# Three moves in a two-layer decoder step: an output panel's upper half between two copies, sample numerators on two column tiles, and the eighth sum of squares with its column sums later

## The chip, the cores and the metric

The kernel runs on one core of a Trainium2 chip, as one launch. The metric is the device time of that launch in microseconds (us); lower is better. One profiled execution gives the durations below; it has its own time, which is not exactly the median of the timed runs.

The engines are named as in the profile: PE (TensorE, with PEld for its weight loads), DVE (VectorE), ACT (ScalarE), POOL (GpSimd) and SP (which here issues DMAs). Each runs its own list of instructions in order and waits on semaphores for the others.

## The reference

Two layers for 512 prompt tokens and 64 sample tokens (8 sequences of 8), model width 1024, in fp32. Layer 0 mixes with multi-head latent attention, layer 1 with a chunkwise mLSTM of 4 heads. Around each mixer stand two half-step feed-forward layers (four in all, width 2816), then a gated per-layer embedding. Cut to what the change touches:

```python
for i in range(DEPTH):                       # 2 layers, both token groups
    x = x + 0.5 * swiglu(rmsnorm(x, g_ffa[i]), w_ffa_in[i], w_ffa_out[i])
    h = rmsnorm(x, g_mix[i])
    x = x + (latent_attention(h) if i == 0 else mlstm(h))
    x = x + 0.5 * swiglu(rmsnorm(x, g_ffb[i]), w_ffb_in[i], w_ffb_out[i])
    gate = sigmoid(rmsnorm(x, g_ple[i]) @ w_ple_gate[i])
    x = x + gate * (p[i] @ w_ple_proj[i])

# swiglu:  a, b = split(h @ w_in); (silu(a) * b) @ w_out
# rmsnorm: x * rsqrt(mean(x * x) + 1e-6) * g
# mlstm, per head, for the 8 sample sequences b of 8 tokens each:
#   num = (S * decay) @ [v, 1] + (q * decay_b) @ [C_b, n_b]     # 64 tokens x 257
```

The last line is what part B below is about: each sample sequence has its own state of 128 x 257, and its 8 tokens alone meet it.

## The kernel before

**Layout.** Tokens lie along the free axis (T = 576), channels on the 128 partitions in 8 chunks. Every fp32 product of weights and activations is made of three: weights and activations are split into an upper half (a rounding to fp32r, made by ACT's `Copy`) and a remainder (`raw - upper`, made by DVE or POOL), and PE multiplies upper x upper, upper x remainder and remainder x upper (lines 2461, 2463, 2466 for panels; 2523, 2524, 2525 for the blocks of the feed-forward's input product).

**Feed-forward.** `Part` cuts the 22 column chunks of the hidden width into three parts (6, 8 and 8 chunks), for each of four feed-forwards. For one chunk `pair(...)` on PE makes seven block products (`block_product`, 12 multiplications of 288 columns each) that form the gate and the value column tile by a Strassen-like scheme; `w_done` counts them. Between them ACT copies intermediate sums from one PSUM bank to another (`copied`, four for a chunk, after block products 1, 2, 3 and 5); the seventh block product waits for the fourth copy, the fifth for the third. Behind the sixth DVE adds and scales (L2181, L2184), ACT takes the silu (L1844), DVE multiplies the two halves (L2169), ACT makes the upper half of the result (L1837) and DVE the remainder (L2173).

After the last chunk of a part come the part's eight output tiles (`out_tile`): tile k needs panel `part.p + k` of `w_out` in its two halves, `whi` (ACT, L1794 through `upper`) and `wlo` (POOL for k = 0 and 1, L1739; DVE for the others). `raw` has 4 slots for panels as they come from memory, `whi` and `wlo` have 2 each. ACT's queue in the part's last chunk, before: copy 1, upper half of the chunk before, copy 2, copy 3, copy 4, then the upper half of panel 0 (it waits for its load, `raw_ready`, and for the slot), then the silu. The upper half of panel 1 stands behind the silu and the last chunk's upper half.

**Between a mixer or the embedding and the next feed-forward** (`added`, and `ple` of layer 0), DVE adds each of 8 tiles to x, prepares the blocks of x for the block products (`x_blocks`) and adds ACT's squares into `acc` (`x_sum`, L2114); four third remainders (`x_third_lower`, L2290) and the fourth weight block's (`fourth_lower`, L2161) end it. PE needs the third remainders in block product 5. `token_sums` on PE (L2474, five columns, ten passes) sums `acc` over the partitions when all eight sums are in; DVE's `means` (L2091), POOL's power (L1750) and PE's `spread` (L2482, after block product 7) make the norm of it.

**mLSTM heads.** For each of 4 heads PE runs four prompt numerators (L1563), a gate panel (24 x 2 multiplications; not in the last head), the stabilisers (L1532 to L1534), the sample numerators (L1573 and L1575), then states (L1582), the prompt state (L1589), the next head's scores (L1548) and turns. DVE copies each numerator (L1404), makes the denominators and carries the states (L1409); ACT squares the copied numerators (L1248) behind the next head's exponentials (L1229, L1231).

In `qdm` each of the 8 sequences has a block of 64 columns, in which only its own 8 tokens are not zero: sequence b has tokens 8b to 8b + 7. A multiplication of one block with state `Cb[:, b, :]` adds into all 64 partitions of the bank, 56 of them zeros.

The functions that the diff touches:

## Time and profile before

| | us |
|---|---|
| median of 3 runs | 2567.34 (2565.26 to 2567.75) |
| the profiled execution | 2565.75 |
| its span | 2563.8 |
| PE busy | 2473.5 (96%) |
| DVE busy | 1684.0 (66%) |
| ACT busy | 1073.0 (42%) |
| POOL busy | 307.7 (12%) |

The granted clock of PE was 0.989 of full speed on the mean, and DMA moved 84 GB/s. The profile's page gives shares over the whole span, the chain of waits follows the end of the program back to its start, and the timeline shows the instructions of one engine in order: start, duration, engine, line, operation, what is written and read, and in brackets how long the engine stood idle before it and what ended that. Equal instructions that follow each other are one row (x16); the duration of a multiplication's row runs to its modelled end, so the step from one row's start to the next is the time that it took.

### The profile page before, as it was taken

What the parts mean: (1) busy time and instruction counts of PE and PEld (TensorE: products, weight loads), DVE (VectorE), ACT (ScalarE), POOL (GpSimd) and SP (SyncE); (2) the same over time, 40 slices, a digit from 0 to 9 for tenths busy, and PEclk for the clock granted to TensorE, in tenths of its full rate; (3) what the DMA queues carried; (4) which work ended last, traced back from release to release, by engine and by line L of the source; (5) the groups of instructions that cost most, each with busy time, mean ns of one, the idle gap of its engine ahead of it and who ended that gap; (6) DMA issues with size and microseconds to landing.
All of it is one profiled execution on the core that took longest, in us unless ns stands there. A gap on an engine that the chain in (4) does not pass through costs nothing.

```text
span 2563.8 us, 45161 instructions
## 1 busy us (share of the span) xinstructions
PE 2473.5 (96%) x17653; PEld 2355.3 (92%) x17653; DVE 1684.0 (66%) x2398; ACT 1073.0 (42%) x1780; POOL 307.7 (12%) x247
## 2 busy tenths in 40 slices
PE   6999999999899999999998999999999999999998
PEld 5999999877688999999998999999997789999998
DVE  6676675888555586848568585765434586857666
ACT  6444353455333453525445353443133354443532
POOL 0000001202330100000030000001322200000012
PEclk9999999999899999999999999999999999999999
DMA  4233232222232222333222333332323222332322
GB/s 121 83 99 91 83 94 78 52 49 75 72 110 77 58 79 87 99 87 94 84 78 78 91 91 91 90 91 71 92 69 103 87 66 82 99 99 82 96 76 72
DMA packets 410806, 216.44 MB, mean 84 GB/s; under 512 B 40085, under 2 KB 407834, under 8 KB 410650
## 3 DMA queue, kind: packets, MB, share of 16 engines
q1 hardware_dynamic: 404646, 209.17, 29.0%
q10 hardware_dynamic: 2420, 3.37, 0.4%
q0 software_dynamic: 3584, 1.84, 0.4%
q8 instruction: 95, 1.56, 0.2%
q14 instruction: 61, 0.50, 0.1%
HBM read 206.57 MB, written 7.76 MB: 84 GB/s over the span
## 4 chain that ended last, share of the span: by engine, by line
PE 87%; DVE 7%; ACT 3%; issue 2%; POOL 1%; DMA 0%; SPq 0%; ACTq 0%; DVEq 0%; POOLq 0%
PE ps L2461 13%; PE ps L2463 13%; PE ps L2466 13%; PE ps L2523 12%; PE ps L2524 12%; PE ps L2525 12%; PE ps L1010 2%; DVE st L628 1%; PE ps L924 1%; POOL wlo L1739 1%; PE ps L886 1%; PE ps L875 1%; PE ps L1563 1%; PE ps L972 1%; PE ps L994 1%
## 5 line engine op out<-in xcount | busy, mean ns | idle before, releaser
L1739 POOL TENSOR_TENSOR wlo<-raw,whi 128x1024 fp32r<-128x1024 f32 (+2 forms) x96 | 207.6, 2163 | 1823.0 <-ACT whi L1794 1823.0
L1794 ACT ACTIVATE whi<-raw 128x1024 fp32r<-128x1024 f32 (+2 forms) x175 | 169.4, 968 | 433.1 <-PE ps L2466 432.1
L2461 PE MATMUL ps<-uh,whi 128*128 128x320 f32 (+1 forms) x1408 | 302.2, 296 | 8.0 <-POOL wlo L1739 7.3
L2463 PE MATMUL ps<-ul,whi 128*128 128x320 f32 (+1 forms) x1408 | 301.1, 295 | 0.0
L2466 PE MATMUL ps<-uh,wlo 128*128 128x320 f32 (+1 forms) x1408 | 301.1, 295 | 0.0
L2461 PEld LDWEIGHTS ps<-uh,whi 128*128 128x128 f32 x1408 | 215.9, 188 | 10.7 <-issue 10.5
L2228 DVE TENSOR_TENSOR ub<-ps,r 128x576 f32<-128x576 f32 x96 | 72.7, 757 | 230.7 <-PE ps L2466 215.0
L2466 PEld LDWEIGHTS ps<-uh,wlo 128*128 128x128 f32 x1408 | 216.0, 188 | 0.0
L2463 PEld LDWEIGHTS ps<-ul,whi 128*128 128x128 f32 x1408 | 216.0, 188 | 0.0
L2147 DVE TENSOR_TENSOR wlo<-raw,whi 128x1024 fp32r<-128x1024 f32 x88 | 107.8, 1225 | 130.3 <-ACT whi L1814 130.3
L2461 PE MATMUL ps<-xh,whi 128*128 128x320 f32 x752 | 164.2, 300 | 3.3 <-DVE RB L1280 2.7
L2463 PE MATMUL ps<-xl,whi 128*128 128x320 f32 x752 | 160.6, 295 | 0.0
L2466 PE MATMUL ps<-xh,wlo 128*128 128x320 f32 x752 | 160.4, 295 | 0.0
L1844 ACT ACTIVATE sA<-tA 128x576 f32<-128x576 f32 x88 | 60.4, 686 | 238.5 <-DVE tA L2184 238.5
L1833 ACT ACTIVATE ps<-ps 128x288 f32<-128x288 f32 x264 | 104.3, 395 | 108.3 <-PE ps L2525 107.6
L1822 ACT ACTIVATE g3h<-g3f 128x1024 fp32r<-128x1024 f32 x88 | 93.5, 1062 | 92.1 <-DVE g3f L2141 87.9
L2181 DVE TENSOR_TENSOR ps<-ps,p 128x576 f32<-128x576 f32 x88 | 66.9, 760 | 85.5 <-PE ps L2525 74.0
L2461 PEld LDWEIGHTS ps<-xh,whi 128*128 128x128 f32 x752 | 115.9, 189 | 4.6 <-DVE RB L1280 2.9
L2523 PE MATMUL ps<-xAh,whi 128*128 128x288 f32 x352 | 106.6, 303 | 12.0 <-issue 12.0
L2463 PEld LDWEIGHTS ps<-xl,whi 128*128 128x128 f32 x752 | 115.9, 189 | 0.0
L2466 PEld LDWEIGHTS ps<-xh,wlo 128*128 128x128 f32 x752 | 115.7, 189 | 0.0
L2523 PE MATMUL ps<-xTh,g3h 128*128 128x288 f32 x352 | 104.3, 296 | 5.2 <-DVE xTl L2290 3.7
(425 smaller groups left out, 7085.3 us busy)
## 6 DMA issues: line engine op xcount, KB each, us to landing
raw<-in_w_ffa_in SPq DMA_DIRECT2D x88, 512.0 KB
raw<-in_w_ffb_in SPq DMA_DIRECT2D x88, 512.0 KB
raw<-in_w_ffa_out SPq DMA_DIRECT2D x32, 512.0 KB
pages<-in_cache_ckv SPq DMA_DIRECT2D x128, 128.0 KB, 2.0
raw<-in_w_ffb_out SPq DMA_DIRECT2D x32, 512.0 KB
raw<-in_w_mlstm_in SPq DMA_DIRECT2D x24, 512.0 KB
raw<-in_w_ple_gate SPq DMA_DIRECT2D x16, 512.0 KB
raw<-in_w_ffa_out SPq DMA_DIRECT2D x16, 384.0 KB
```

The costliest lines, as they stand in the source:

```text
L1739: pool.tensor_tensor(lo[:, 0:n, :], raw[:, p % RAW, 0:n, :], hi[:, 0:n, :].bitcast(F32), ALU.subtract).then_inc(wlo_ready, 1)
L1794: act.activation(hi[:, 0:n, :], raw[:, p % RAW, 0:n, :], ACT.Copy).then_inc(whi_ready, 1)
L1822: act.activation(flat_g(g3h, i), flat_g(g3f, i), ACT.Copy).then_inc(g_hi, 1)
L1833: act.activation(dst, src, ACT.Copy).then_inc(w_copied, 1)
L2147: dve.tensor_tensor(wlo[:, s, :, :], raw[:, 2 * part.half(i), :, :], whi[:, s, :, :].bitcast(F32), ALU.subtract).then_inc(g_lo, 1)
L2228: dve.tensor_tensor(ub[:, :], slot(part.t + c, bank), r[:, :], ALU.mult).then_inc(out_read, 1)
L2461: mm(out[:, t], hi[:, n, :], xh_n[:, t], start=first and n == 0, stop=False)
L2463: mm(out[:, t], hi[:, n, :], xl_n[:, t], start=False, stop=False)
L2466: ins = mm(out[:, t], lo[:, n, :], xh_n[:, t], start=False, stop=end)
L2523: mm(out, w_h, m_h, start=fresh and n == 0, stop=False, skip_group_check=not fresh)
L2524: mm(out, w_h, m_l, start=False, stop=False, skip_group_check=not fresh)
L2525: ins = mm(out, w_l, m_h, start=False, stop=n == 3, skip_group_check=not fresh)
```

## The change

It has three parts. (A) In the last chunk of each part ACT makes the upper half of output panel 0 ahead of the fourth copy, not behind it. (B) The sample numerators are written in two halves of the bank's 64 partitions: 0 to 31 for sequences 0 to 3 and 32 to 63 for 4 to 7, in turn; each stationary tile has 32 columns in place of 64. (C) In the stages ahead of feed-forwards 1, 2 and 3, DVE adds the eighth square behind the third and fourth remainders, and PE makes the column sums behind block product 5 in place of 4.

```diff
--- before.py
+++ after.py
@@ -1569,10 +1569,14 @@
                 pe.wait_ge(l_SD, NTT * (h + 1))
                 pe.wait_ge(l_in, h + 1)
                 pe.wait_ge(l_nu, 5 * h + 3)
-                out = ps[0:TS, B5, 0:DV + 1]
-                mm(out, SD[h % 2][0:TS, 1280:1280 + TS], Vt[0:TS, 4, h, :], start=True, stop=False)
-                for b in range(NB):
-                    ins = mm(out, qdm[:, b * TS:(b + 1) * TS], Cb[:, b, :], start=False, stop=b == NB - 1)
+                half = TS // 2
+                for o in (0, half):
+                    mm(ps[o:o + half, B5, 0:DV + 1], SD[h % 2][0:TS, 1280 + o:1280 + o + half], Vt[0:TS, 4, h, :],
+                       start=True, stop=False)
+                for k in range(NB // 2):
+                    for b, o in ((k, 0), (k + NB // 2, half)):
+                        ins = mm(ps[o:o + half, B5, 0:DV + 1], qdm[:, b * TS + o:b * TS + o + half], Cb[:, b, :],
+                                 start=False, stop=k == NB // 2 - 1)
                 ins.then_inc(l_num, 1)
 
             def states(h, b):
@@ -1872,14 +1876,14 @@
                             second_upper(part, i + 1)
                         if more:
                             third_upper(part, i + 1)
+                        if not more:
+                            act.wait_ge(w_done, 7 * (g - 1) + 4)
+                            upper(part.p, 0, part.n)
                         copied(part, i, 4, 5, D_, B)
                         if embed:
                             embed_square(4)
                         if i == 0 and part.q == 0:
                             r_copy(FFNS[f], 1)
-                        if not more:
-                            act.wait_ge(w_done, 7 * (g - 1) + 4)
-                            upper(part.p, 0, part.n)
                         if i or part.q:
                             gate(part, i)
                     u_upper(part, part.n - 1)
@@ -2302,7 +2306,7 @@
                     if c == 7 and f:
                         third_lower(PART[f][0], 0)
                     x_block_lower(f, c - 4)
-                    if f:
+                    if f and c < 7:
                         x_sum(FFNS[f], c)
 
             def added(name, f):
@@ -2324,6 +2328,7 @@
                 for k in range(4):
                     x_third_lower(f, k)
                 fourth_lower(part, 0)
+                x_sum(FFNS[f], 7)
 
             def ple(l, nxt):
 
@@ -2385,6 +2390,7 @@
                     for k in range(4):
                         x_third_lower(2, k)
                     fourth_lower(part, 0)
+                    x_sum(FFNS[2], 7)
                     return
                 c0 = v["chain"]
                 proj(0, 0, 0, p0 + 2, t0 + 4, 0, c0, 0)
@@ -2567,11 +2573,11 @@
                               False, False, need(5, 2))
                 block_product(whi[:, s, :, :], wlo[:, s, :, :], 4, lambda n: xBh[:, n, 0:HT], lambda n: xBl[:, n, 0:HT], A,
                               False, True, need(6, 2))
-                if new and f:
-                    token_sums(0)
                 pe.wait_ge(w_copied, 4 * g + 3 + dyn * 4)
                 block_product(g2h[:, e, :, :], g2l[:, e, :, :], 0, lambda n: xTh[:, n, 1, :], lambda n: xTl[:, n, 1, :], B,
                               False, True, need(13, 1))
+                if new and f:
+                    token_sums(0)
                 block_product(g3h[:, e, :, :], g3l[:, e, :, :], 4, lambda n: xBh[:, n, HT:T], lambda n: xBl[:, n, HT:T], C,
                               False, True)
                 pe.wait_ge(g_hi, part.uppers(i, 4) + add)
```

In the rows of the changed kernel below the line numbers are 4 to 6 higher for the same code.

**ACT, last chunk of the first part.** `ps<-ps` and `p_90<-ps` are the copies, `whi<-raw` the output panels' upper halves, `sA<-tA` the silu, `uh<-ub` the gated product's upper half. Before:

```order
L1829 ACTIVATE g4h<-raw 128x512
L1833 ACTIVATE ps<-ps 128x288
L1837 ACTIVATE uh<-ub 128x576
L1833 ACTIVATE p_90<-ps 128x288
L1833 ACTIVATE ps<-ps 128x288 x2
L1794 ACTIVATE whi<-raw 128x768
L1844 ACTIVATE sA<-tA 128x576
L1837 ACTIVATE uh<-ub 128x576
L1794 ACTIVATE whi<-raw 128x768 x7
```

and now:

```order
L1833 ACTIVATE g4h<-raw 128x512
L1837 ACTIVATE ps<-ps 128x288
L1841 ACTIVATE uh<-ub 128x576
L1837 ACTIVATE p_90<-ps 128x288
L1837 ACTIVATE ps<-ps 128x288
L1798 ACTIVATE whi<-raw 128x768
L1837 ACTIVATE ps<-ps 128x288
L1848 ACTIVATE sA<-tA 128x576
L1841 ACTIVATE uh<-ub 128x576
L1798 ACTIVATE whi<-raw 128x768 x7
```

The first output panel's upper half went up by one row: it stands between the third and the fourth copy, and the silu follows the fourth copy.

**PE, first head, from the stabilisers to the states.** `Vt` and `SDa` are values and weighted scores, `Cb` the states and `qdm` the decayed queries. Before:

```order
L1532 MATMUL ps<-RB,cf 128x512
L1533 MATMUL ps<-RB,cf 128x64
L1534 MATMUL ps<-RE,cf 128x72
L1573 MATMUL ps<-Vt,SDa 64x257
L1575 MATMUL ps<-Cb,qdm 64x257 x8
L1582 MATMUL ps<-Vt,kwb 128x257 x4
L1589 MATMUL ps<-Vt,kw 128x257 x4
L1582 MATMUL ps<-Vt,kwb 128x257 x4
```

and now:

```order
L1532 MATMUL ps<-RB,cf 128x512
L1533 MATMUL ps<-RB,cf 128x64
L1534 MATMUL ps<-RE,cf 128x72
L1574 MATMUL ps<-Vt,SDa 32x257 x2
L1578 MATMUL ps<-Cb,qdm 32x257 x8
L1586 MATMUL ps<-Vt,kwb 128x257 x4
L1593 MATMUL ps<-Vt,kw 128x257 x4
L1586 MATMUL ps<-Vt,kwb 128x257 x4
```

Nine multiplications into 64 partitions became ten into 32; the eight with `Cb` alternate between partitions 0 to 31 and 32 to 63. What stands around them is the same.

**DVE, end of the stage ahead of feed-forward 1.** `xBl` is the last block's remainder, `acc` the sum of squares, `xTl` the third remainders, `g4l` the fourth weight block's, `g2f` belongs to the next chunk. Before:

```order
L2157 TENSOR_TENSOR g3l<-g3f,g3h 128x1024
L2285 SCALAR_TENSOR_TENSOR xBl<-x,gn,xBh 128x576
L2114 TENSOR_TENSOR acc<-acc,sq 128x576
L2290 TENSOR_TENSOR xTl<-xTf,xTh 128x576 x4
L2161 TENSOR_TENSOR g4l<-raw,g4h 128x512
L2129 SCALAR_TENSOR_TENSOR g2f<-raw 128x1024
L2147 TENSOR_TENSOR wlo<-raw,whi 128x1024
```

and now:

```order
L2161 TENSOR_TENSOR g3l<-g3f,g3h 128x1024
L2289 SCALAR_TENSOR_TENSOR xBl<-x,gn,xBh 128x576
L2294 TENSOR_TENSOR xTl<-xTf,xTh 128x576 x4
L2165 TENSOR_TENSOR g4l<-raw,g4h 128x512
L2118 TENSOR_TENSOR acc<-acc,sq 128x576
L2133 SCALAR_TENSOR_TENSOR g2f<-raw 128x1024
L2151 TENSOR_TENSOR wlo<-raw,whi 128x1024
```

The addition into `acc` went down behind `g4l`; on PE the five multiplications with `acc` (ten passes) went down by one block product of 12.

## Rows read from the trace of the kernel before

**Rows 1.** The page, part 4: shares of the chain that ended last, by engine.

```profile
PE 87%; DVE 7%; ACT 3%; issue 2%; POOL 1%; DMA 0%; SPq 0%; ACTq 0%; DVEq 0%; POOLq 0%
```

**Rows 2.** Waits of PE: who for whom, us in total, times, longest.

```profile
PE ps L2461 <- POOL wlo L1739: 7.9, 9, 0.9
```

**Rows 3.** Timeline of PE, end of a part of 8 chunks (start, duration, instruction, [idle before]).

```profile
238.99 0.29 PE L2523 MATMUL ps<-xTh,g4h 128*128 128x288 f32 x1
...
239.25 0.29 PE L2525 MATMUL ps<-xTh,g4l 128*128 128x288 f32 x1
240.47 0.50 PE L2461 MATMUL ps<-uh,whi 128*128 128x320 f32 x2 [0.92 <-POOL wlo L1739]
...
241.34 0.43 PE L2461 MATMUL ps<-uh,whi 128*128 128x320 f32 x2
...
242.13 0.43 PE L2461 MATMUL ps<-uh,whi 128*128 128x320 f32 x2
```

**Rows 4.** Timeline of ACT at the same place.

```profile
233.18 0.40 ACT L1833 ACTIVATE ps<-ps 128x288 f32<-128x288 f32 x1 [1.12 <-PE ps L2525]
236.38 0.40 ACT L1833 ACTIVATE ps<-ps 128x288 f32<-128x288 f32 x1 [2.81 <-PE ps L2525]
236.69 1.05 ACT L1794 ACTIVATE whi<-raw 128x1024 fp32r<-128x1024 f32 x1
...
241.67 1.04 ACT L1794 ACTIVATE whi<-raw 128x1024 fp32r<-128x1024 f32 x1
```

**Rows 5.** Timeline of POOL at the same place.

```profile
237.82 2.39 POOL L1739 TENSOR_TENSOR wlo<-raw,whi 128x1024 fp32r<-128x1024 f32 x1 [122.11 <-ACT whi L1794]
242.79 2.40 POOL L1739 TENSOR_TENSOR wlo<-raw,whi 128x1024 fp32r<-128x1024 f32 x1 [2.58 <-ACT whi L1794]
```

**Rows 6.** DMA rate from 219 to 231 us, in 40 slices of 0.3 us.

```profile
GB/s 0 0 0 0 0 0 0 138 147 324 352 352 340 347 299 285 292 290 248 84 0 0 0 0 0 0 0 0 0 0 0 0 0 0 0 0 0 0 0 0
```

**Rows 7.** Timeline of POOL, end of a part of 6 chunks.

```profile
113.87 1.85 POOL L1739 TENSOR_TENSOR wlo<-raw,whi 128x768 fp32r<-128x768 f32 x1 [3.13 <-ACT whi L1794]
```

**Rows 8.** Timeline of PE's weight loads at the same place, output tile 1.

```profile
115.83 0.30 PEld L2461 LDWEIGHTS ps<-uh,whi 128*128 128x128 f32 x2
```

**Rows 9.** Timeline of PE, first mLSTM head.

```profile
1919.29 0.65 PE L1573 MATMUL ps<-Vt,SDa 64*64 64x257 f32 x2
1919.87 3.69 PE L1575 MATMUL ps<-Cb,qdm 128*64 128x257 f32 x16
1923.49 1.56 PE L1582 MATMUL ps<-Vt,kwb 64*128 64x257 f32 x6
```

**Rows 10.** The sample numerators' line: duration in ns min/median/max.

```profile
L1575 PEld LDWEIGHTS ps<-Cb,qdm x64: 132/136/139, 1919.9 to 2019.1; 128*64 128x64 f32 x64
L1575 PE MATMUL ps<-Cb,qdm x64: 377/379/432, 1919.9 to 2019.3; 128*64 128x257 f32 x64
```

**Rows 11.** Timeline of PE in the attention layer, two 64-wide column tiles in turn.

```profile
502.90 2.37 PE L886 MATMUL ps<-PT,Vp 128*64 128x512 f32 x16
505.21 0.44 PE L832 MATMUL ps<-cf,raw 128*128 128x128 f32 x2
```

**Rows 12.** Timeline of DVE, first mLSTM head.

```profile
1924.68 1.26 DVE L1409 SCALAR_TENSOR_TENSOR Cb<-Cb,dec,ps 128x257 f32<-128x257 f32 x3
```

**Rows 13.** Timeline of ACT, first mLSTM head.

```profile
1922.32 0.64 ACT L1229 ACTIVATE SDb<-Md,cols 128x128 f32<-128x128 f32 x2
```

**Rows 14.** Timeline of PE, first chunk of feed-forward 1.

```profile
905.86 1.17 PE L2474 MATMUL ps<-cf,acc 128*128 128x1 f32 x10
...
911.11 0.37 PE L2523 MATMUL ps<-xTh,g4h 128*128 128x288 f32 x1 [0.77 <-ACT ps L1833]
```

**Rows 15.** Timeline of DVE at the same place.

```profile
901.94 0.76 DVE L2114 TENSOR_TENSOR acc<-acc,sq 128x576 f32<-128x576 f32 x1
902.61 2.77 DVE L2290 TENSOR_TENSOR xTl<-xTf,xTh 128x576 fp32r<-128x576 f32 x4
...
909.49 0.16 DVE L2091 TENSOR_SCALAR rq<-ps 128x5 f32<-128x5 f32 x1
```

## The prediction

> **What bounds the kernel now.** I read the page's chain of work first, then the waits of PE, then the timeline at each place that the diff touches, and last the source and DMA views for what those places rest on. PE holds 87% of the chain that ended last [rows 1]; no other engine's time counts unless PE waits for it. Among PE's waits the one this change can reach is that of the output panels (L2461) for POOL's remainder: 7.9 us in 9 stretches [rows 2], of which the timeline shows eight of 0.92 us at the ends of feed-forward parts of eight column chunks. In the mLSTM heads PE stands still for little, so what is shortened there is PE's own work.
>
> **Part A, the upper half of an output panel between two copies.** There are 12 parts (4 feed-forward layers, 3 each), eight with 8 chunks and four with 6. The part that ends at 239.4 us shows what happens. The last block product's last triple starts at 238.99, its third multiplication at 239.25, so one takes 0.13 and the first output tile could start at 239.38; it starts at 240.47. It is also slow to get going: its first step to the next chunk is 0.87, later ones 0.79 [rows 3]. That is 1.09 + 0.08 = 1.17 us a part. The timeline prints only 0.92 as idle, because it models the last multiplication's end late. The cause: ACT makes the upper half at 236.69 for 1.05, behind the fourth copy [rows 4], and POOL needs 2.39 from 237.82, until 240.21 [rows 5]; PE starts 0.2 later. The timeline shows nothing else that holds tile 0.
>
> Now the upper half stands behind the third copy (first row of [rows 4]), which ends at 233.58. It starts there at once if its weights have landed: the burst that brings them (1.05 MB in the window, which is panels 0 and 1) is over at about 225 us, 8 us earlier [rows 6]. So upper half 233.5 to 234.6, POOL 234.6 to 237.0, and tile 0 has its operands 2.2 us before 239.4. The fourth copy waits for a product and ran at 236.38 (second row of [rows 4]); ACT is free again at 234.6, well before it is due. ACT's queue behind it (silu, gated product's upper half) waits for DVE, not for the slot that became free. The panel for RAW slot 0 is fetched 3.2 us earlier; DMA is idle then or has room.
>
> What is late next is panel 1. Its upper half comes on ACT behind the last silu and the gated product (241.67), POOL's remainder at 242.79 for 2.40, until 245.19 [rows 4, 5]; this chain hangs on the block products, which do not move. Tile 1 would want it at 246.86 - 1.17 = 245.7 (eight steps after tile 0): 0.4 in hand. In the layers where a step is 0.78 the same sum leaves 0.2. In a part of 6 chunks tile 0 lasts only 4.8, and there POOL's second remainder (113.87 + 1.85 = 115.72) already decides: PE's load for tile 1 starts at 115.83, 0.1 behind it [rows 7, 8]. So what tile 0 wins in those four parts (0.3 each) is lost again at tile 1. **A = 8 x 1.17 = -9.4 us.** Ends: 0 if tile 1 or the copy takes over everywhere, -10.6 with 0.3 for each short part.
>
> **Part B, sample numerators on column tiles.** Per head PE spends 1919.29 to 1923.49 = 4.20 us on 9 multiplications, of which 8 (16 passes, fp32 goes in two) take 3.62: 0.226 a pass [rows 9]. All stream 257 columns into 64 partitions of the bank. Now there are 10 multiplications into 32 partitions each, 20 passes, taken in turn for partitions 0 to 31 and 32 to 63. The trace has no pair of such 32-wide tiles, but it has a pair of 64-wide ones: L886 writes partitions 0 to 63 and 64 to 127 of one bank in turn, 16 passes with 5120 columns. At L1575's rate (3.62 us for 4112 columns) these would need 4.51 one after another; from 502.90 to the next line's start at 505.21 they take 2.31 [rows 11]. So two tiles overlap with a factor of 1.95, in fp32, with a weight load at each pass, in one bank. 20 passes x 0.226 / 1.95 = 2.32; gain 1.88 a head, 4 heads. I round down for the switch of tile sizes: 1.85. Ends: factor 2 gives 2.26 (-7.8 in all); no overlap 4.52 (+1.3).
>
> The Trainium skill (TensorEngine Tiling, Overview and Performance Considerations) says that column tiling applies to 32 output columns too. Its page TensorE: Matmul & The Clock Gate, Part 3, measured 2.38 for three such tiles; at the same share of the ideal two would give 1.6, and B would be about -5.5. No run here shows 32-wide pairs; L886's row is nearer in everything but the width.
>
> Does a wait take it back? Behind the numerators stand DVE's copy, three small operations, and the carries of the state from 1924.68; all of them hang on PE's last pass and come 1.85 earlier. The only other input in that stretch is ACT's row of squares, which waits for the next head's exponentials; these end at 1922.96 and do not move [rows 12, 13]. DVE asks for the squares after three carries, at 1922.83 + 1.26 = 1924.1; that leaves ACT 1.1 for one row of 256 squares. So the cover holds, and PE's later waits for carries keep their size. The next gate panel and its remainder are ready long before, and the last head's numerators wait for DVE behind the earlier ones. **B = 4 x 1.85 = -7.4 us.**
>
> **Part C, the eighth sum of squares last, its column sums a product later.** Three places (feed-forwards 1, 2, 3). On DVE one addition, 0.67 from its start to the next, goes from ahead of the four third remainders and the fourth to behind them. The remainders ran from 902.61 for 2.77 [rows 15], and PE asked for them only when the ten column-sum passes that start at 905.86 were over, after 1.04 [rows 14]. Now PE asks at 905.86, and they begin at 901.94: the last is ready at 904.7. The sum is ready at about 906.0; PE now wants it at 905.86 and 12 multiplications of 0.13, 907.5. Both fit, and PE's order costs the same passes. The next consumer of the column sums, DVE's mean, runs at 909.49 behind four block operations; the sums will end near 908.5, so 0.9 in hand. And PE waits at 911.11 for a copy that stands on ACT behind an upper half made from DVE's block sums, which do not move [rows 14]: anything PE won before it would be lost there. **C = 0.** Ends: -2.0 if 3 x 0.67 came through, +2.0 if a late sum pushed the same.
>
> Sum against the profiled execution, which took 2565.75 (span 2563.8): -9.4 - 7.4 = -16.8, to 2549.0. The median of the three runs is 2567.34, 1.6 above it; I forecast against the median: **2550.5 us**.
>
> **Rivals.** (1) *The tiles run one after another.* 20 passes x 0.226 = 4.52, +0.3 a head; with A the time is 2567.3 - 9.4 + 1.3 = 2559.2. For: no 32-wide pair in the trace. Against: L886.
> (2) *Weight loads stand open between column tiles.* A load takes 0.136 [rows 10]. Ten slots of 0.226 and 20 loads make 4.98, +0.8 a head: 2567.3 - 9.4 + 3.1 = 2561.0. Against: L886 would then take over 4 us. The Trainium skill speaks for this one (TensorE: Matmul & The Clock Gate, Part 3): a load runs beside multiplications in flight only when the row group differs, and here it is the same. By that rule L886's 2.31 could not be; the trace disagrees.
> (3) *A's wait moves.* The copy or panel 1's remainder takes its place in the long parts too: A = 0, time 2559.9. For: tile 1's margin of 0.2 to 0.4, and the four short parts, where this is so already. Against: the sums above.
> (4) *Slower: the array empties at each change of tile.* Then each of 20 passes stands alone with load and full length, 0.136 + 0.379 [rows 10] = 0.515, 10.3 a head against 4.20, +24.4 in all: 2567.3 - 9.4 + 24.4 = 2582.3. It decides from 0.33 us a pass on: there 80 passes cost the 16.8 of the old ones and the 9.4 of A. Against: L886 alternates at each chunk without a trace of it.
>
> **Chances.** Forecast 82%, with its own range 2547.5 to 2553.5; rival 1 5%, rival 2 3%, rival 3 7% (with its halves), rival 4 3%. Range 2546.5 to 2560: the forecast, B by the page's factor, and rivals 1 and 3. A measurement of this kernel tells about 0.2% (5 us) from no change. All cases but the fourth and mishaps near zero lie below 2562.2: faster 93%, within 4%, slower 3%.
>
> **What will show it.** A: the row PE L2461 <- POOL falls from 7.9 to about 0.6 (the panel behind the attention layer's norm stays), POOL's first remainder of each part starts some 3 us ahead, tile 0's first step follows the last block product by 0.13; short parts gain nothing. B: from the first numerator pass to the first state product 2.3 to 2.5 instead of 4.20, and DVE's carries as much earlier. C: the column sums stand behind the next block product, and PE's stall of 0.77 before the fourth weights' product keeps its size. Wrong would be: an idle gap at tile 1 of the long parts, a longer stall ahead of the next head's scores, or 20 passes over 4 us.

## The result and the profile after

The changed kernel takes 2542.61 us (median of 4 runs, 2540.62 to 2545.19) against 2566.30 for the kernel before beside it: ratio 0.9909, 95% interval 0.9892 to 0.9926. It is 23.7 us faster where 16.8 were forecast. Its profiled execution took 2545.19, with a span of 2543.3.

Parts A and B show much as forecast. PE's waits for POOL's remainder, in total, times and longest, answer to [rows 2]:

```profile
PE ps L2467 <- POOL wlo L1743: 2.4, 6, 0.6
```

Four of the six are 0.33 us at tile 1 of the short parts; none is in a long part. The other two are 0.60 us behind the attention layer's norm and 0.45 us in the input products of the mLSTM layer. The end of the part shown in [rows 3], on PE:

```profile
237.86 0.29 PE L2529 MATMUL ps<-xTh,g4h 128*128 128x288 f32 x1
...
238.12 0.29 PE L2531 MATMUL ps<-xTh,g4l 128*128 128x288 f32 x1
238.26 0.43 PE L2467 MATMUL ps<-uh,whi 128*128 128x320 f32 x2
```

Tile 0 follows the last block product by 0.14 us, where 1.22 stood (239.25 to 240.47). ACT at the same place, beside [rows 4]:

```profile
232.06 0.40 ACT L1837 ACTIVATE ps<-ps 128x288 f32<-128x288 f32 x1 [1.12 <-PE ps L2531]
232.36 1.05 ACT L1798 ACTIVATE whi<-raw 128x1024 fp32r<-128x1024 f32 x1
235.26 0.40 ACT L1837 ACTIVATE ps<-ps 128x288 f32<-128x288 f32 x1 [1.84 <-PE ps L2531]
```

POOL there, beside [rows 5]:

```profile
233.49 2.39 POOL L1743 TENSOR_TENSOR wlo<-raw,whi 128x1024 fp32r<-128x1024 f32 x1 [118.06 <-ACT whi L1798]
241.67 2.39 POOL L1743 TENSOR_TENSOR wlo<-raw,whi 128x1024 fp32r<-128x1024 f32 x1 [5.79 <-ACT whi L1798]
```

The upper half stands between the copies, and the remainder is ready at 235.88, 2.4 us before tile 0 wants it. In the short parts the second remainder decides, as in [rows 7, 8]:

```profile
115.58 0.50 PE L2467 MATMUL ps<-uh,whi 128*128 128x320 f32 x2 [0.33 <-POOL wlo L1743]
```

Part B, PE in the first mLSTM head, beside [rows 9]:

```profile
1905.03 0.41 PE L1574 MATMUL ps<-Vt,SDa 64*32 64x257 f32 x2
...
1907.13 0.38 PE L1578 MATMUL ps<-Cb,qdm 128*32 128x257 f32 x2
1907.44 0.48 PE L1586 MATMUL ps<-Vt,kwb 64*128 64x257 f32 x1
```

From the first numerator to the first state product it is 2.41 us in place of 4.20, and so in the second and third head. In the fourth the granted clock fell to half (1.2 GHz) at 1997 us, amid the numerators, and they took 3.16 us in this profile. Part C, the wait ahead of the fourth weights' product, beside [rows 14]:

```profile
908.08 0.37 PE L2529 MATMUL ps<-xTh,g4h 128*128 128x288 f32 x1 [0.76 <-ACT ps L1837]
```

It keeps its size. By the records' start times the gap ahead of tile 0 fell from 1.21 to 0.13 us, and the first step of tile 0, against the next one, is longer by 0.01 us where it was by 0.07. At full clock in all four heads the three parts give 8 x 1.14 + 4 x 1.79 = 16.3 us. The rest is in a view that the prediction does not draw on: PE's output products by shape. Before (line, instruction, count, busy us, mean ns of one, idle before):

```profile
L2461 PE MATMUL ps<-uh,whi 128*128 128x320 f32 x704 | 218.4, 310 | 8.0 <-POOL wlo L1739 7.3 <-issue 0.7
...
L2461 PE MATMUL ps<-uh,whi 128*128 128x256 f32 x704 | 198.0, 281 | 0.0
```

After:

```profile
L2467 PE MATMUL ps<-uh,whi 128*128 128x320 f32 x704 | 213.4, 303 | 1.3 <-POOL wlo L1743 1.3
...
L2467 PE MATMUL ps<-uh,whi 128*128 128x256 f32 x704 | 197.8, 281 | 0.0
```

The same 704 multiplications of 320 columns became 7 ns shorter on the mean, though nothing in them was edited; those of 256 did not. Where this is, equal windows over four of the eight long parts' output stretches tell (window, its length, PE's busy time and products, granted clock, DMA share and GB/s). Before:

```profile
243.00:288.00 45.00, 45.00 (x339) 1.00 0.28 83
385.00:430.00 45.00, 45.00 (x340) 1.00 0.32 84
...
1104.00:1149.00 45.00, 45.00 (x349) 1.00 0.29 84
1245.00:1290.00 45.00, 45.00 (x348) 1.00 0.25 75
```

After:

```profile
241.00:286.00 45.00, 45.00 (x349) 1.00 0.28 82
381.00:426.00 45.00, 45.00 (x348) 1.00 0.31 82
...
1099.00:1144.00 45.00, 45.00 (x348) 1.00 0.28 82
1239.00:1284.00 45.00, 45.00 (x349) 1.00 0.24 74
```

PE is busy all the time at full clock in every row, yet it issues 339 or 340 products in some and 348 or 349 in others. The records' start times say how: a pair of products (320 and 256 columns) follows the pair before by 0.267 us in the stretches with 339 or 340, and by 0.260 in those with 348 or 349; nearly every stretch keeps its cadence to the end. A part is called slow or fast below by this cadence alone. I call the time over 0.260 a pair, summed, the excess. A slow long part has 1.26. In the twelve output stretches it was 8.7 us before (four of eight long parts slow, and the four short ones, wholly or from tile 1 on) and is 0.1 after; over the same pairs of the other stages, outside half clock, it was 5.1 and is 3.5.

Summed for the profiled executions: 16.3 + 8.6 + 1.6 = 26.5 us, against 20.6 measured (2565.75 to 2545.19). What the changed kernel is ahead by shrinks by 2.9 us between 640 and 690 us and by 2.7 between 2000 and 2030, where the stretches of half clock lie otherwise in the two. Within the span 54.2 us were at half clock before and 58.0 after, and PE was busy in 41.1 and 47.5 of them. Half of the 6.4 between these, 3.2 us, is my estimate of what that cost. Half clock falls differently in every execution (54.2 us in this profile of the kernel before, 46.7 in another, e1 below), so I take this part as no work of the change; the other 2.7 of the remainder are not explained.

### The profile page after: what moved, and what is told of

The parts are those of the page before. It is cut to its first block, busy times and chain, and to the rows that moved or that the text cites. A ratio compares the mean times of both kernels' runs of the same rounds, so it can differ in the third digit from the quotient of the medians.

```text
span 2543.3 us, 45177 instructions
## 1 busy us (share of the span) xinstructions
PE 2456.9 (97%) x17661; PEld 2340.3 (92%) x17661; DVE 1684.0 (66%) x2398; ACT 1072.7 (42%) x1780; POOL 307.3 (12%) x247
## 4 chain that ended last, share of the span: by engine, by line
PE 87%; DVE 7%; ACT 3%; issue 2%; POOL 1%; DMA 0%; SPq 0%; DVEq 0%; ACTq 0%; POOLq 0%
PE ps L2467 13%; PE ps L2469 12%; PE ps L2472 12%; PE ps L2529 12%; PE ps L2530 12%; PE ps L2531 12%; PE ps L1010 2%; DVE st L628 1%; PE ps L924 1%; PE ps L886 1%; PE ps L875 1%; PE ps L1563 1%; PE ps L972 1%; PE ps L994 1%; PE ps L973 1%
## 5 line engine op out<-in xcount | busy, mean ns | idle before, releaser
L2467 PE MATMUL ps<-uh,whi 128*128 128x320 f32 (+1 forms) x1408 | 296.8, 292 | 1.3 <-POOL wlo L1743 1.3
```

What stands on the lines that cost most here:

```text
L2467: mm(out[:, t], hi[:, n, :], xh_n[:, t], start=first and n == 0, stop=False)
```

## The experiments

The experiments ran in four groups, and the kernel before ran beside each. Its medians were 2563.7 (e1 to e4), 2567.4 (e5 to e8), 2562.2 (e9 to e12) and 2569.1 us (e13 to e15). A ratio is taken to the kernel before of the same group, with its 95% interval in brackets. The excess and the stalls are read from the one profiled execution of each kernel.

### Each part alone, and nothing at all

e1 is the kernel before, unedited.

> The kernel before, not changed. It is here for PE's cadence: in the trace before, an output product's two spans (320 and 256 columns) follow each other every 0.267 us in the feed-forward parts of layers 0 (both of the first feed-forward's long parts) and of the third feed-forward, and every 0.260 us in the long parts of the second and fourth; in the changed kernel every feed-forward part runs at 0.260. Theory P (the entry into the stream sets the cadence, and the program fixes the entry): the same parts are slow again, about 8.7 us too much in the twelve parts. Theory R (each execution draws its own cadence, whatever the kernel): other parts are slow this time, and the sum differs by several us. Time the same as before within 0.1% by both.

Measured: 2565.23, ratio 1.0004 (0.9995 to 1.0014). The excess is again large (9.2 in the twelve parts), but other parts are slow: five of eight long ones, three of which were fast in the first profile, while two that were slow there are fast here. So the slow cadence does not belong to a layer; it is drawn anew in each execution.

e2 has part A alone:

```diff
+                        if not more:
+                            act.wait_ge(w_done, 7 * (g - 1) + 4)
+                            upper(part.p, 0, part.n)
                         copied(part, i, 4, 5, D_, B)
...
-                        if not more:
-                            act.wait_ge(w_done, 7 * (g - 1) + 4)
-                            upper(part.p, 0, part.n)
```

> Part A alone. By the terms of the prediction (eight stalls of 1.17 us go, nothing else): -9.4 us, 2557. Theory P: with the stall gone the stream is entered without a break, all twelve parts run at 0.260, and another 8 to 9 us go: -17 to -18, about 2549. Theory R: -9.4, and the cadence of the parts is as mixed as in the unchanged kernel.

Measured: 2548.38, ratio 0.9938 (0.9921 to 0.9954), that is 0.0062 of 2563.7, 15.9 us. All twelve parts are fast, excess 0.1. A alone brings 15.9 (by the interval 11.8 to 20.3) where its stalls are 9.4, the stages that B and C touch left as they were.

e3 has part B alone:

```diff
-                    ins = mm(out, qdm[:, b * TS:(b + 1) * TS], Cb[:, b, :], start=False, stop=b == NB - 1)
...
+                        ins = mm(ps[o:o + half, B5, 0:DV + 1], qdm[:, b * TS + o:b * TS + o + half], Cb[:, b, :],
+                                 start=False, stop=k == NB // 2 - 1)
```

> Part B alone. Prediction's term: 4 x 1.85 = -7.4 us, 2559; from the first numerator pass to the first state product 2.3 to 2.5 us instead of 4.20. Theory P: the cadence of the parts ahead of the heads (first three feed-forwards) is as in the unchanged kernel; that of the fourth feed-forward may differ, by at most 1.3 a part. Theory R: mixed anywhere.

Measured: 2558.17, ratio 0.9976 (0.9967 to 0.9986), -6.2 us (3.6 to 8.5 by the interval). Its first head:

```profile
1915.49 0.62 PE L1574 MATMUL ps<-Vt,SDa 64*32 64x257 f32 x4
1916.04 1.93 PE L1578 MATMUL ps<-Cb,qdm 128*32 128x257 f32 x16
1917.90 0.48 PE L1586 MATMUL ps<-Vt,kwb 64*128 64x257 f32 x1
```

2.41 again. Two long parts are slow, and the short ones wholly or in part (excess 6.2): B does nothing for the cadence.

e4 has part C alone:

```diff
-                if new and f:
-                    token_sums(0)
                 pe.wait_ge(w_copied, 4 * g + 3 + dyn * 4)
...
+                if new and f:
+                    token_sums(0)
```

with the eighth sum on DVE moved behind the remainders.

> Part C alone. Prediction's term: 0 us. The stall of 0.77 before the fourth weight block's product stays. Theory P: since the column sums and a block product swap places ahead of three feed-forwards, the entries behind may be another phase, but each feed-forward part still starts after POOL's stall; at most a few us either way. A rival for the missing gain: C is worth some us by itself; then this run is 3 us or more faster.

Measured: 2561.99, ratio 0.9997 (0.9988 to 1.0007): no change. The excess is 7.3, with three long parts slow. A and B alone bring 15.9 + 6.2 = 22.1, the whole change 23.7.

### Is it the stall? A stall put back, and what ends it

e5 is the changed kernel with a stall of another origin ahead of tile 0:

```diff
-                    pe.wait_ge(w_ub, part.g0 + part.n - 1)
+                    pe.wait_ge(w_ub, part.g0 + part.n)
```

> The changed kernel, all three parts, but PE waits ahead of output tile 0 for the last chunk's gated product (one count more on the semaphore w_ub) and not for the last but one. The panel's two halves are ready early as in the changed kernel, so POOL and ACT work where part A put them; only PE stands still, about 1.8 us in each of twelve parts. Theory P+R, from the first four runs (a stream entered without a break always runs at 0.260 per pair of spans; one entered after a stall draws 0.260 or 0.267 and keeps it): the stalls cost 12 x 1.9 = +23 us against the changed kernel, and the cadence is mixed again, some 3 to 9 us above 0.260 over the twelve parts. Rival (it is ACT's and POOL's place, work beside the stream, that slows it): +23 us, and all twelve parts stay at 0.260, under 0.3 us in sum.

Measured: 2560.95, ratio 0.9974 (0.9964 to 0.9984). PE's wait:

```profile
PE ps L2467 <- DVE ub L2173: 18.7, 12, 1.6
```

All twelve parts stayed fast. "Any stall brings the slow cadence" fell. The time is 18.3 us over the changed kernel's, less than the 23 of the expectation: the gap ahead of tile 0 grew by 1.72 us in twelve places, 20.7, and the four stalls at tile 1 of the short parts (1.3) went.

e9 brings POOL's stall back and leaves ACT in its new order:

```diff
                     for k in (0, 1):
+                        if k == 0:
+                            pool.wait_ge(w_done, 7 * (part.g0 + part.n - 1) + 6)
                         lower(part.p + k, 0, part.n)
```

> The changed kernel, but in every feed-forward part POOL also waits for the last block product of the part before it computes its first remainder, as the remainder's buffer made it wait before the change; ScalarE's copies keep their new order. The stall of 0.92 us before tile 0 of the eight long parts should be back, and again be ended by POOL (some 1.1 us each, 8 x 1.1 = 9 us by the stall alone). Theory 1: a stall that POOL ends draws the cadence of the products behind it; then some of the eight long parts run at 0.267 us a pair again (several of the 24 stretches with an excess of 1.26 us), and the time is about 2542.6 + 9 + some 6 = 2557 to 2559. Theory 2: the slow cadence came from ScalarE's place, the upper half copied beside the first products; then all twelve parts stay at 0.260 and the time is 2551 to 2553.

Measured: 2558.82, ratio 0.9988 (0.9978 to 0.9999). PE stalls for POOL again:

```profile
240.97 0.50 PE L2469 MATMUL ps<-uh,whi 128*128 128x320 f32 x2 [1.11 <-POOL wlo L1743]
```

and the same windows over the long parts show both cadences:

```profile
1103.00:1148.00 45.00, 45.00 (x340) 1.00 0.29 86
1246.00:1291.00 45.00, 45.00 (x349) 1.00 0.25 74
...
1576.00:1621.00 45.00, 45.00 (x348) 1.00 0.29 84
1717.00:1762.00 45.00, 45.00 (x339) 1.00 0.34 84
```

Excess 5.7 in the twelve parts: three long parts and two short ones are slow. ACT's copy beside the first products, which stays where the change put it, was not the cause; the stall is.

e11 is the kernel before with e5's edit: POOL and ACT in their old places, but DVE ends the stall.

> The kernel before the change, but TensorE also waits for VectorE's write of ub before tile 0 of every feed-forward part, as in the kernel with the stall put back. POOL and ScalarE keep their old places; only the last release before tile 0 is now VectorE's, about 0.7 us after POOL's in the eight long parts: by the stalls alone about 2566 + 8 x 0.7 + 4 x 1.6 = 2578. Theory 1 (who ends the stall matters): all twelve parts fast, the excess over 0.260 us a pair in them falls from 8.7 to 9.2 us to near 0, and the time is near 2578 - 9 = 2569. Theory 2 (POOL's or ScalarE's work beside the first products matters): the excess stays at 6 to 9 us and the time is near 2578.

Measured: 2568.46, ratio 1.0023 (1.0011 to 1.0034). All twelve parts fast, excess 0.0, in the kernel before. The gaps between the last block product and tile 0 grew by 8 x 0.64 + 4 x 1.40 = 10.7 us, while the medians differ by 6.3 and the profiled execution (2565.93) is as long as that of the kernel before (2565.75): the cadence paid for much of the stall. (1.5 us of this comparison is another matter: ahead of the mLSTM layer's input products PE waited 2.68 us for DVE in the profile of before and 1.19 for POOL in e11's. Both lengths occur without an edit, 2.68 in the kernel before and 1.19 in e1.)

e10 makes DVE's stall longer:

```diff
-                    pe.wait_ge(w_ub, part.g0 + part.n - 1)
+                    pe.wait_ge(u_ready, part.g0 + part.n)
```

> The changed kernel, but TensorE waits before tile 0 of every feed-forward part until VectorE has finished the block inverse's u itself, a stall of some 3.9 us in 12 places that VectorE ends: 2542.6 + 12 x 3.9 = 2589 by the stall alone. Theory 1 (who ends the stall matters): all twelve parts stay at the fast cadence, excess near 0, and the time is 2586 to 2592. Theory 2 (the length of the stall matters, 1.6 us was lucky): some parts fall to 0.267 us a pair, each such stretch with 1.26 us more, and the time is up to 12 us above that.

Measured: 2599.95, ratio 1.0161 (1.0140 to 1.0181), more than either theory said.

```profile
PE ps L2467 <- DVE ul L2177: 36.8, 12, 3.1
```

Two of twelve parts were slow, so DVE's end is not safe by itself. And the clock came in, in windows around one of the twelve:

```profile
380.00:385.00 5.00, 5.00 (x40) 1.00 0.52 138
385.00:388.00 3.00, 0.40 (x4) 1.00 0.31 93
388.00:392.00 4.00, 3.53 (x15) 0.57 0.02 4
392.00:400.00 8.00, 8.00 (x64) 1.00 0.23 66
```

Behind this stall PE runs at half clock, 1.2 GHz, until about 392. All eight long parts have such a stretch. In all 95.8 us of the span were at half clock, against 54.5 in e12, the changed kernel of the same group, and PE was busy in 80.5 and 44.3 of them; half of the difference, 18.1 us, is the estimate of what the clock cost. The gaps are longer by 12 x 3.23 = 38.8 by the records' start times, the excess by 2.0, and the short parts' stalls at tile 1 (1.3) are gone: 57.6 us in all, where the two profiled executions differ by 55.4. I had left the clock out of the expectation.

e12 is the changed kernel once more:

> The changed kernel once more, unedited, for its cadence and ratio on the chip of this call. Every theory expects a ratio near 0.991 (2541 to 2545 us). Theory 1: the excess over 0.260 us a pair in the twelve feed-forward parts is again under 1 us, for no long part stalls on POOL; if the cadence were a matter of chance in every part, some of the 8 long parts would now be slow, with 1.26 us more a stretch.

Measured: 2543.87, ratio 0.9932 (0.9915 to 0.9948); all twelve parts fast.

### Which engine, or which length?

e13 makes POOL wait one block product longer than e9:

```diff
-                            pool.wait_ge(w_done, 7 * (part.g0 + part.n - 1) + 6)
+                            pool.wait_ge(w_done, 7 * (part.g0 + part.n))
```

> The changed kernel, but POOL waits for the very last block product of a feed-forward part before its first remainder, 0.40 us later than in the kernel with POOL late: POOL ends a stall whose gap from product to product is about 1.80 us in the eight long parts (1.25 in the short ones), as long as VectorE's of 1.85 that left all twelve parts fast. Theory 1 (the engine that ends the stall decides, since POOL's end falls anywhere against TensorE's steps): some long parts are slow, an excess of 3 to 8 us, and the time is 2543.9 + 8 x 1.67 + 4 x 0.8 + 3 to 8 = 2563 to 2568. Theory 2 (the length decides): all eight long parts are fast, and the time is 2558 to 2561.

Measured: 2591.44, ratio 1.0082 (1.0058 to 1.0106). I had priced a block product at 0.40 us, the spacing of its triples; it has four of them, 1.6. So the gap was 3.0 us in the long parts and not 1.8, the clock fell here too (0.984 on the mean; a stretch of half clock in seven of the eight long parts), and three of eight long parts and all short ones were slow. It says nothing on a stall of 1.85.

e14 and e15 put ACT's and DVE's ends ahead of tile 0 of the changed kernel:

```diff
+                    pe.wait_ge(silu_done, part.g0 + part.n)
                     pe.wait_ge(w_ub, part.g0 + part.n - 1)
```

(e15: `pe.wait_ge(w_act, 2 * (part.g0 + part.n))` in its place.)

> The changed kernel, but TensorE waits before tile 0 of every feed-forward part until ScalarE has written the last sA, which is about 1.3 us after the last block product: a stall like POOL's of before in length, in twelve places, ended by ScalarE. Theory 1 (POOL is what draws): all twelve parts fast, excess under 0.5 us, time 2543.9 + 12 x 1.1 = 2557. Theory 2 (any stall of about 1.2 us draws): four or five of the twelve parts slow, excess 3 to 8 us, time 2560 to 2565.

Measured: 2550.41, ratio 0.9926 (0.9900 to 0.9952). All twelve fast, with a gap of 1.06 between block product and tile 0, nearly POOL's of before (1.21). The time is 6.5 us over e12's median where 13 were expected; the gaps account for 12 x 0.93 less 1.3 at tile 1, 9.9, and the two profiled executions differ by 7.8. The interval here is wide (6.7 us either way).

> The changed kernel, but TensorE waits before tile 0 of every feed-forward part until VectorE has written the last tA, about 0.6 us after the last block product: a stall shorter than POOL's of before, in twelve places, ended by VectorE. Theory 1 (POOL is what draws): all twelve parts fast, excess under 0.5 us, time 2543.9 + 12 x 0.55 = 2550 or 2551. Theory 2 (short stalls draw, those of 1.85 us do not): several of the twelve parts slow, excess 3 to 8 us, time 2553 to 2558.

Measured: 2551.45, ratio 0.9933 (0.9911 to 0.9956). Five of twelve slow, four of the long ones, with an excess of 6.0; the time is the first theory's, the cadence the second's:

```profile
383.00:428.00 45.00, 45.00 (x348) 1.00 0.31 82
...
1101.00:1146.00 45.00, 45.00 (x339) 1.00 0.28 82
1242.00:1287.00 45.00, 45.00 (x340) 1.00 0.25 74
```

So neither the engine nor the length alone decides. In two of the kernels the records' nanoseconds separate the parts. In e15 the gap was 0.346 or 0.347 us ahead of all seven parts with a cadence of 0.260, and 0.344 or 0.345 ahead of the five with 0.267. In e9's long parts, which POOL's stall precedes, it was 1.402 or 1.403 ahead of the five with 0.260 and 1.405 ahead of the three with 0.267. In the others they do not: in the kernel before gaps of 1.210 us stand ahead of three fast long parts and a slow one, over before, e1, e3 and e4 gaps of 1.212 ahead of both kinds, in e10 slow and fast parts share 3.360 and 3.361, and in e13 2.977 stands ahead of a fast and a slow one. DVE's 1.85 and ACT's 1.06 repeated within 3 ns in all their parts and were always fast; POOL's of before spread from 1.207 to 1.369 and were mixed. So the length of the gap alone, even to the nanosecond, does not tell what cadence follows. Entries into tile 0, counted over all profiles:

| how tile 0 is entered | entries | slow |
|---|---|---|
| without a break (A in: after, e2, e6, e7, e8, e12) | 72 | 0 |
| after POOL's stall, long parts (before, e1, e3, e4, e9) | 40 | 17 |
| the same, short parts | 20 | 13 |
| DVE ends it, gap 1.85 (e5, e11) | 24 | 0 |
| ACT ends it, gap 1.06 (e14) | 12 | 0 |
| DVE ends it, gap 0.35 (e15) | 12 | 5 |
| DVE ends it, gap 3.4 (e10) | 12 | 2 |
| POOL ends it, gap 3.0, in short parts 2.4 (e13) | 12 | 7 |

What is counted is the cadence in tile 0. In some short parts it changes at tile 1; of the sixteen stalls of 0.33 there with A in (after, e2, e8, e12) one, e8's last, was followed by the slow cadence.

### Two further versions, and the tiles in another order

e6 also moves panel 1's upper half, behind the fourth copy:

```diff
                         copied(part, i, 4, 5, D_, B)
+                        if not more:
+                            upper(part.p + 1, 0, part.n)
...
-                    upper(part.p + 1, 0, part.n)
```

> The changed kernel with the upper half of panel 1 early too, right behind the fourth copy of the last chunk (in place of behind the last chunk's own upper half). The four short parts lose their stall of 0.33 at tile 1 (with the slower first step 0.4 each): -1.6 us against the changed kernel, 2541. The row PE output product <- POOL shows only the stall behind the attention input's norm, 0.6. Rival: the silu, which stands behind it now, is late and the gated product with it; then tile 0's last chunk waits and nothing is won.

Measured: 2539.96, ratio 0.9901 (0.9883 to 0.9919). The stalls at tile 1 of the short parts are gone. That the kernel is faster by it is not shown by the times: the interval overlaps the changed kernel's (0.9892 to 0.9926). PE's wait for POOL:

```profile
PE ps L2468 <- POOL wlo L1743: 1.8, 2, 1.2
```

Beside the 0.60 that was expected it holds 1.20 ahead of the mLSTM layer's input products, in place of 2.68 for DVE and 0.45 for POOL in the changed kernel's profile. That is the wait of two lengths noted at e11 and no effect of this edit that I can show.

e7 is e6, and in the first chunk of each feed-forward it puts the fourth copy ahead of the third upper half on ACT:

```diff
-                        if more:
+                        first = i == 0 and part.q == 0
+                        if more and not first:
                             third_upper(part, i + 1)
...
+                        if first:
+                            third_upper(part, i + 1)
```

> As e6, and in each feed-forward's first chunk the fourth copy stands ahead of the third upper half on ACT. PE stands still for 0.76, 0.86 and 1.21 us ahead of the seventh block product of feed-forwards 1 to 3 for that copy. If the copy alone holds PE: these go, -2.8, less what the norm's root on POOL (2.0 us from the column sums' mean) then makes late: about -2 against e6. Rival: DVE's order sets both, and the wait moves to the spread or to the next chunk's remainders: 0.

Measured: 2539.24, ratio 0.9895 (0.9877 to 0.9913). PE's wait for those copies, which was 7.6 us in 12 stretches in the changed kernel:

```profile
PE ps L2533 <- ACT ps L1837: 4.1, 9, 0.6
```

The stalls of 0.76 to 1.21 are gone. Against e6 the median fell by 0.7 us only, within the noise, where 2 were expected, and the profiled executions are equal (2538.78 and 2538.92); but e7's has the long waits ahead of the mLSTM layer (2.68 and 0.45) and e6's the short one (1.20), a difference of 1.9. So whether the copy ahead gains its 2 us is not settled. The median is 3.4 us below the changed kernel's, and the lowest of all, but the two intervals overlap: that e7 is faster than the changed kernel is likely by the rows, and not shown by the times.

e8 is the changed kernel with the numerators of one column tile after those of the other:

```diff
-                for k in range(NB // 2):
-                    for b, o in ((k, 0), (k + NB // 2, half)):
+                for o in (0, half):
+                    for k in range(NB // 2):
+                        b = k + (NB // 2 if o else 0)
```

> The changed kernel, but the sample numerators' eight state products go first all to partitions 0 to 31, then all to 32 to 63, in place of in turn. Same count and size. If the overlap of two column tiles is what part B lives from (theory), passes into one tile follow each other at 0.226: from first numerator pass to first state product about 4.3 us in place of 2.41, +7.5 us in four heads. Rival: narrow tiles are faster by themselves; then 2.4 stays and the time is that of the changed kernel.

Measured: 2547.25, ratio 0.9926 (0.9908 to 0.9944), 4.6 us over the changed kernel's median, though the intervals overlap. The first head:

```profile
1902.46 0.62 PE L1574 MATMUL ps<-Vt,SDa 64*32 64x257 f32 x4
1903.01 2.83 PE L1579 MATMUL ps<-Cb,qdm 128*32 128x257 f32 x16
1905.77 0.48 PE L1587 MATMUL ps<-Vt,kwb 64*128 64x257 f32 x1
```

3.31 us for 20 passes in place of 2.41, 0.9 more a head and 3.6 in all, where 1.9 more a head were expected. Passes into one tile are not faster for being narrow: among the records' start times are two rows of eight, in steps of 0.241 first and then 0.216 to 0.221 us, as in the 64-wide numerators of [rows 9] (0.215 to 0.221). The second row starts at 1903.913, 0.90 us behind the first (1903.013), when that still has four passes to start. The same in equal windows (in brackets the passes under way in each, those begun earlier too):

```profile
1903.00:1903.88 0.88, 0.87 (x4) 1.00 0.00 0
1903.88:1904.76 0.88, 0.88 (x9) 1.00 0.00 0
1904.76:1905.64 0.88, 0.88 (x6) 1.00 0.00 0
```

Four, eight and four passes start in the three. The two rows can only be the two tiles, for in program order the first tile has all its eight passes ahead of the second's. So PE started the second tile's passes beside the first tile's last four, and taking turns was worth the other four places, 4 x 0.22 = 0.9 us. The expectation of 4.3 had no overlap at all. One short part was slow here from tile 1 on, where its POOL stall of 0.35 is.

## Why the prediction was wrong

The forecast was 2550.5; the time is 2542.6, outside the range.

**Part A, the stall: right.** 1.22 to 0.14 ahead of tile 0, eight times, and a first step of 0.79 against 0.78; the short parts lose it again at tile 1, as said. The wait for POOL came out at 2.4 and not 0.6: the four stalls of 0.33 that the prediction had itself put at tile 1 were missing from its row, and 0.45 at the mLSTM layer's input products.

**Part A, the sum: the step that failed.** "It is also slow to get going: its first step to the next chunk is 0.87, later ones 0.79 ... That is 1.09 + 0.08 = 1.17 us a part", and "A = 8 x 1.17". The later steps were taken as given. I had both cadences before me ("In the layers where a step is 0.78") and took them for a property of the layers; the two profiles of the kernel before (the first and e1) show that it is not. The stall that A removes also drew the cadence of the 144 or 192 pairs behind it. What A's term left out measured 8.6 us in the profiles; with it, -9.4 - 8.6 - 7.4 on 2567.3 is 2541.9. This term is a draw: in the four profiles with the old stall (before, e1, e3, e4) the excess was 6.2 to 9.2. e2 confirms it (A alone 15.9, with 9.4 outside its interval), e9 from the other side: its gaps are longer than e12's by 8 x 1.27 + 4 x 0.73, less the four stalls at tile 1, which makes 11.8; with 5.7 of excess 17.5. The profiled executions differ by 18.1, the medians by 15.0.

**Part B: right.** 2.41 for 2.32 forecast, 7.2 us at full clock for 7.4; alone 6.2 measured. The overlap factor is 4.52 / 2.41 = 1.88, against 1.95 from [rows 11]. Its premise, 0.226 for a pass into one tile whatever its width, holds by e8 (0.216 to 0.221 from pass to pass). Rivals 1, 2 and 4 (4.52, 4.98 and 10.3 a head) are out. The Trainium skill (TensorE: Matmul & The Clock Gate, Part 3) has weight loads run beside multiplications only where the row group differs. The trace disagrees: the row group is the same here, and 20 loads of 0.11, 2.2 us, leave no room in 2.41 for multiplications that wait for them.

**Part C: right**, nothing gained or lost, alone or in the whole.

**Rival 3** did not come: no idle gap at tile 1 of any long part. Its mechanism is in the short parts alone, and e6 takes it out.

**The range** had no case below 2546.5: the best ends that I had priced for the three parts (-10.6, -7.8 and -2.0) together give 2546.9. A cost that lies in the running products behind a stall had no term.

## What to carry to other kernels

Count the instructions in equal windows where the bounding engine is busy without a gap, at the same clock: if they differ between repeats of the same code, a stall ahead of them may be costing more than its idle time. A gapless hand-over to a long stream of multiplications can be worth more than the gap; here it was 15.9 us for 9.4. When a cost seems to belong to a layer, look whether a second execution gives it to the same one.

## What the runs showed of the hardware that I had not expected

- Two cadences of back-to-back products at full clock, 0.260 and 0.267 us for a pair of 320 and 256 columns: 2.6% of such a stretch, with PE busy in both. Entered without a break (gap 0.13) tile 0 was always fast, 72 times of 72. After a stall the cadence varied between executions of one kernel, and mostly kept to the next break. Neither the releasing engine nor the length of the stall decides by itself, and gaps equal to the nanosecond were followed by both cadences. What decides, and why the slow one persists, stays open. It was not tried to shift one release by single ns.
- A gap of 3.0 to 3.4 us ahead of the output products (e13, e10) brought a stretch of half clock (1.2 GHz) behind it in seven and in eight of the eight long parts; gaps up to 1.85 us (e5, e11) did so in none.
- Two column tiles of 32 in turn overlap in fp32 with a factor of 1.88 (20 passes in 2.41 us, at 0.226 each 4.52). Without taking turns they overlap too, in part: in e8 the second tile's first pass started while four of the first tile's eight were still to start, and 20 passes took 3.31 us. Passes into one tile followed each other by 0.22 us at 32 columns as at 64. Their weight loads were shorter, a median of 0.110 us against 0.136 in [rows 10], which did not change that step.
